# The second layer's input projection in Strassen pairs only, its right side made during the output tiles

## The reference, cut to what matters

```python
h = rms_norm(x, norm_g)
c_q, c_kv, k_rope, z = jnp.split(
    h @ w_in, [Q_LORA, Q_LORA + KV_LORA, Q_LORA + KV_LORA + QK_ROPE], axis=-1)   # 768, 256, 32, 1024 columns
q = (rms_norm(c_q, q_lat_g) @ w_uq).reshape(B, S, MLA_HEADS, QK_HEAD)
...
k = jnp.concatenate([k_nope, jnp.broadcast_to(k_rope[:, :, None, :], ...)], axis=-1)
q = rope_tail(rms_norm(q, q_head_g), cos, sin)
k = rope_tail(rms_norm(k, k_head_g), cos, sin)
o = causal_attention(q, k, v)
return x + (o * jax.nn.silu(z)) @ w_out
```

## Time and profile before

| what | us |
|---|---|
| median of 3 runs | 961.72 (961.34 to 962.45) |
| span of the profiled execution | 960.9 |
| PE busy | 947.5 |
| DVE busy | 812.9 |
| ACT busy | 575.2 |
| POOL busy | 353.1 |

### The profile page before, as it was taken

One profiled execution on the slowest core, in us unless ns is written; L12 is line 12 of the kernel. 1 busy time (PEld: TensorE's weight loads), 2 busy tenths in 40 slices (PEclk: granted clock), 3 DMA queues, 4 the chain that ended last, 5 costly groups with the idle time before them and its releaser, 6 DMA issues.

```text
span 960.9 us, 17257 instructions
## 1 busy us (share of the span) xinstructions
PE 947.5 (99%) x6406; PEld 671.3 (70%) x6406; DVE 812.9 (85%) x1410; ACT 575.2 (60%) x1076; POOL 353.1 (37%) x393
## 2 busy tenths in 40 slices
PE   9999999999999999999999999998999999999998
PEld 8788544444688887644457999996788888887443
DVE  5798899899865579988887899998999999998763
ACT  6443544424434454454646888866899989997230
POOL 0002233222000002235412577875652478894220
PEclk9999999999999999999999999999999999999999
DMA  9320422111054422332123264566676775460231
GB/s 305 45 61 23 110 77 56 44 45 45 1 175 155 152 67 67 107 112 58 31 72 111 89 205 150 204 181 176 119 163 145 171 150 122 82 179 2 88 110 65
DMA packets 165347, 103.74 MB, mean 108 GB/s; under 512 B 75272, under 2 KB 149520, under 8 KB 165008
## 3 DMA queue, kind: packets, MB, share of 16 engines
q1 hardware_dynamic: 159216, 102.25, 38.0%
q10 hardware_dynamic: 6048, 0.39, 0.5%
HBM read 56.48 MB, written 29.36 MB: 89 GB/s over the span
## 4 chain that ended last, share of the span: by engine, by line
PE 72%; DVE 19%; POOL 3%; issue 3%; ACT 2%; DVEq 0%; POOLq 0%; ACTq 0%
PE banks L111 19%; PE banks L113 19%; PE banks L112 19%; PE banks L2728 7%; PE banks L2746 2%; PE banks L2748 2%; PE banks L2747 2%; DVE heads_y L2480 1%; POOL heads_prod L2616 1%; DVE heads_x L2476 1%; DVE heads_x L2475 1%; DVE front_lt L1223 1%; DVE heads_ss L2522 1%; PE banks L2756 1%; DVE front_l L1223 1%
## 5 line engine op out<-in xcount | busy, mean ns | idle before, releaser
L2497 DVE TENSOR_TENSOR heads_pt_lo<-banks,heads_pt_hi 128x512 f16<-128x512 f32 (+2 forms) x192 | 102.1, 554 | 10.8 <-ACT heads_pt_hi L2360 7.8
L2360 ACT ACTIVATE heads_pt_hi<-banks 128x512 f16<-128x512 f32 (+2 forms) x192 | 89.1, 487 | 9.1 <-PE banks L2728 8.9
L2748 PE MATMUL banks<-heads_v,heads_pt_lo 128*128 128x64 f16 x576 | 71.1, 194 | 0.0
L2747 PE MATMUL banks<-heads_v,heads_pt_hi 128*128 128x64 f16 x576 | 71.0, 194 | 0.0
L2489 DVE CUSTOM_DVE_ANT_0 heads_probs_big<-banks,heads_mask,score_scale 128x1024 f32<-128x1024 f32 (+1 forms) x64 | 68.6, 1072 | 2.9 <-PE banks L113 2.7
L2746 PE MATMUL banks<-heads_v,heads_pt_hi 128*128 128x64 f16 x576 | 70.9, 194 | 0.0
L2728 PE MATMUL banks<-ident,heads_probs_big 128*128 128x128 f32 x416 | 69.5, 281 | 1.2 <-ACT heads_probs_big L2351 1.1
L2351 ACT ACTIVATE heads_probs_big<-heads_probs_big,heads_neg_max 128x1024 f32<-128x1024 f32 (+1 forms) x64 | 63.4, 990 | 8.8 <-DVE heads_neg_max L2489 7.7
L111 PE MATMUL banks<-heads_k_t,heads_q_t 96*128 96x512 f16 (+2 forms) x192 | 63.0, 328 | 1.0 <-DVE heads_neg_max L2489 1.0
L111 PE MATMUL banks<-front_act_hi,front_w_hi 128*128 128x512 f32 x160 | 63.8, 399 | 0.0
L113 PE MATMUL banks<-front_act_hi,front_w_lo 128*128 128x512 f32 x160 | 62.4, 390 | 0.0
(11 more groups left out here) (489 smaller groups left out, 3114.5 us busy)
## 6 DMA issues: line engine op xcount, KB each, us to landing
qk_scratch<-heads_y SPq DMA_DIRECT2D x22, 512.0 KB, 3.7
front_x<-in_x_t SPq DMA_DIRECT2D x16, 512.0 KB, 5.3
front_raw<-in_w_in_ab SPq DMA_DIRECT2D x14, 512.0 KB, 5.1
qk_scratch<-heads_last_y SPq DMA_DIRECT2D x10, 512.0 KB, 3.8
front_w<-in_w_out_ab SPq DMA_DIRECT2D x8, 512.0 KB, 3.9
x_scratch<-front_x SPq DMA_DIRECT2D x8, 512.0 KB, 3.9
v_scratch<-heads_v SPq DMA_DIRECT2D x32, 128.0 KB, 3.0
heads_v_st<-v_scratch SPq DMA_DIRECT2D x8, 512.0 KB, 5.2
```

The costliest lines, as they stand in the source:

```text
L2360: nc.scalar.activation(pt_hi[:, q % PIECES, :width], t_ps[:, banks[("piece", n, k)] % 3, :width], ACT.Copy).then_inc(pt_high, 1)
L2497: nc.vector.tensor_tensor(pt_lo[:, q % PIECES, :width], t_ps[:, banks[("piece", n, k)] % 3, :width], pt_hi[:, q % PIECES, :width], ALU.sub ...
L2747: nc.tensor.matmul(o_part, pt_hi[:, q % PIECES, blk], v2[e][:, j, VH:], start=False, stop=False)
L2748: last = nc.tensor.matmul(o_part, pt_lo[:, q % PIECES, blk], v2[e][:, j, :VH], start=False, stop=(j == i))
```

## The change

All of the gate's tiles are made in pairs: two early gate pairs (8 and 9) stand ahead of the four latent pairs (now 10 to 13), and the last two are 14 and 15. The plain tiles 16 to 20 are gone. The right forms are made during the output tiles, two chunk halves at a time (`MADE_AT`), with POOL making most of their sums. Their scale no longer comes from the largest value but from a bound on it, of the norms of x, y and the output weights, that is known ahead of the output tiles (`weight_norm`, `y_norm`, `later_scaling`, one matmul after tile 9). The token sums and the spread of the roots move into pair 8. The rotary keys are made per 128 tokens by products of the right forms (as weights) with the 32 columns' high and low parts (64 or 32 columns wide), after the fourth product of pair 9 (`rotated_keys`). Row sum 8 stands in tile 14, its maximum behind DVE's work on tile 13. A raw pair is loaded by four DMAs instead of two. Some small tiles move, and the areas of the latents, the gate and the right forms change places.

```diff
-    Z0 = OUT0 + OUT_TILES
-    ROPE0 = Z0 + PLAIN_GATES
-    TILES = ROPE0 + 1
-    GATE_PAIRS = PAIRED + LAT // 2
+    TILES = OUT0 + OUT_TILES
+    LAT0 = PAIRED + EARLY_GATES // 2
+    GATE_PAIRS = LAT0 + LAT // 2
...
+    MADE_AT = {2 * c: [(c, SMALL_PART)] + ([(c - 1, T1_PART + n) for n in (1, 2, 3)] if c else []) + [(c, T1_PART)]
+               for c in range(CHUNKS)}
+    MADE_AT |= {2 * c + 1: [(c, WIDE_PART)] for c in range(CHUNKS - 1)}
+    MADE_AT[NK - 1] = [(CHUNKS - 1, T1_PART + 1), (CHUNKS - 1, WIDE_PART), (CHUNKS - 1, T1_PART + 2), (CHUNKS - 1, T1_PART + 3)]
...  (ACT)
                 snapshot(p, 2)
+                weight_norm(p)
...
+            for k in range(NK):
+                y_norm(k)
...
+        def weight_norm(j):
+            slot = norm_in[j % NORM_SLOTS]
+            act.wait_ge(norm_loaded[j % NORM_SLOTS], 16 * (j // NORM_SLOTS + 1))
+            nc.scalar.activation(slot[:], slot[:], ACT.Square, accum_out=norms[:, NK + j:NK + j + 1]).then_inc(norm_squared, 1)
+        def y_norm(k):
+            act.wait_ge(y_high, NK)
+            if k:
+                act.wait_ge(norm_squared, NK + k)
+            nc.scalar.activation(norm_in[0][:], f32(y_hi[:, k, :]), ACT.Square, accum_out=norms[:, k:k + 1]).then_inc(norm_squared, 1)
...
+        for m in range(OUT_TILES):
+            if m and OUT0 + m + 2 < TILES:
+                high(OUT0 + m + 2)
+            act.wait_ge(evacuated, OUT0 + m + 1)
...
+            nc.scalar.activation(xg_of(m)[:], x1[m % RING][:], ACT.Copy, scale=gam1[:, m:m + 1]).then_inc(xg_ready, 1)
+            if m < NK - 1:
+                x1_square(m)
+            rights(m)
+            if m == OUT_TILES - 2:
+                pair_forms(PAIRED, range(FORMS))
         later_paired()
...  (POOL)
         for p in range(PAIRED):
             left_sums(p)
+        for c in range(CHUNKS - 1):
+            right_sums(c, range(4))
         for p in range(PAIRED, ALL_PAIRS):
             left_sums(p)
+            if p == PAIRED:
+                right_sums(CHUNKS - 1, [0])
...  (DVE)
+        for m in range(OUT_TILES):
+            n, x1_m = OUT0 + m, x1[m % RING]
+            if m == 0:
+                low(n + 2)
+            elif m > 1 and n + 1 < TILES:
                 low(n + 1)
+            dve.wait_ge(x1_in[m % RING], 16 * (m // RING + 1))
+            dve.wait_ge(proj_ready, n + 1)
+            nc.vector.tensor_tensor(x1_m[:], proj[:, ring_bank(n)], x1_m[:], ALU.add).then_inc(evacuated, 1)
+            if m == 0:
+                later_scaling()
+            if m < NK - 1:
+                rights(m)
+                if m:
+                    add_x1_square(m)
             else:
+                last_sums()
+            if m == OUT_TILES - 3:
+                pair_peak(PAIRED)
+            if m == OUT_TILES - 2:
+                pair_scale(PAIRED)
+                pair_low(PAIRED, range(FORMS))
         later_paired()
...
+        def first_later_pair():
+            rights(NK - 1)
+            add_x1_square(NK - 1)
+            pair_peak(PAIRED + 1)
+            roots(2, ms1, rstd1, tmp1, sums[:, 0])
...
+            quarter(PAIRED, 0)
+            quarter(PAIRED, 1)
+            pair_scale(PAIRED + 1)
+            pair_low(PAIRED + 1, range(4))
+            quarter(PAIRED, 2)
+            pair_low(PAIRED + 1, range(4, FORMS))
...  (PE)
+                    if n == OUT0 + OUT_TILES - 2 and c == 0 and k == 2:
+                        row_sum(PAIRED)
...
+            pe.wait_ge(mixed, GROUPS)
+            pe.wait_ge(norm_squared, 2 * NK)
+            nc.tensor.matmul(pooled[:, BANK:BANK + K_ROW + 1], ones[:], norms[:], start=True, stop=True).then_inc(bound_spread, 1)
...
-                    if p + 1 < ALL_PAIRS and i == 2:
+                    if p + 1 < ALL_PAIRS and i == (4 if p == PAIRED else 2):
                         row_sum(p + 1)
+                    if p == PAIRED and i == 2:
+                        pe.wait_ge(x1_added, OUT_TILES - 1)
+                        pe.wait_ge(scale_set, PAIRED + 1)
+                        token_sums()
                     if p == PAIRED and i == 3:
+                        spread_roots(2, sums[:, 0])
+                    if p == PAIRED + 1 and i == 3:
+                        rotated_keys()
...
+            for t in range(NT):
+                half, cols = t * P // BANK, slice(t * P % BANK, t * P % BANK + P)
+                whole = slice(t * P, (t + 1) * P)
+                terms = []
+                for c in range(CHUNKS):
+                    terms += [(later_small[c][:, part, cols], 2 * c, part) for part in range(2)]
+                    if half:
+                        terms += [(later_t1[part][:, c, cols], 2 * c, part) for part in range(2)]
+                    terms += [(later_wide[c][:, part, whole], 2 * c + 1, part) for part in range(2)]
+                for j, (tokens, k, part) in enumerate(terms):
+                    width = ROPE if part else 2 * ROPE
+                    last = nc.tensor.matmul(turned_ps[:, t, :width], tokens, wr[:, k, :width], ...)
```

More of the change, by code:

```diff
@@ L259, in front @@
[L259 to L265, removed]
+    xg = [row(f"xg{n}", place) for n, place in enumerate((7, 9, 5, 8))]
@@ new lines, in front @@
+    forms_at = arena + 16 * ROW
+    later_small = [at(f"l11_{c}", [P, 2, BANK], F16, forms_at + c * (ROW // 2)) for c in range(CHUNKS)]
+    later_wide = [at(f"l2_{c}", [P, 2, S], F16, forms_at + (2 + c) * ROW) for c in range(CHUNKS)]
+    later_t1 = [at(f"lt1_{part}", [P, CHUNKS, BANK], F16, forms_at + (6 + part) * ROW) for part in range(2)]
+    later_t = at("lt", [P, 3, 2, CHUNKS, BANK], F16, forms_at + 8 * ROW)
+    stage = [at(f"stage{n}", [P, BANK], F32, w_place + place * ROW + n % 2 * (ROW // 2)) for n, place in enumerate((10, 10, 1, 1))]
@@ L420, in raw_landed @@
     def raw_landed(eng, p):
-        eng.wait_ge(raw_in[p % 2], 32 * (p // 2 + 1) + (0 if p % 2 else 32))
+        loads = sum(4 if q == 0 or q >= PAIRED else 2 for q in range(p % 2, p + 1, 2))
+        eng.wait_ge(raw_in[p % 2], 16 * loads)
     def left_sum(p, n):
@@ L869, in later_paired @@
                 if p == PAIRED:
-                    plain_silu(PLAIN_GATES - 1)
+                    x1_square(NK - 1)
+                if LAT0 <= p < LAT0 + 2:
+                    for i in range(2):
+                        early_silu(2 * (p - LAT0) + i)
                 if p == GATE_PAIRS - 1:
@@ L1243, in plain_gate, with last_sums, add_x1_square @@
-        def plain_gate(i):
-            dve.wait_ge(proj_ready, Z0 + i + 1)
+        def last_sums():
+            dve.wait_ge(xg_ready, NK)
+            dve.wait_ge(t_added, STAGED0 + 4 * (CHUNKS - 1) + 1)
+            for n in (1, 2, 3):
+                t_sum(dve, nc.vector, CHUNKS - 1, n)
+        def add_x1_square(m):
+            dve.wait_ge(x1_squared, m + 1)
+            if m > 1:
+                dve.wait_ge(x1_added, m - 1)
+            nc.vector.tensor_tensor(sums[:, 0], sums[:, 0], x1_sq[:], ALU.add).then_inc(x1_added, 1)
@@ L1429, in vector @@
-        later_scaling()
-        low(Z0 + 1)
-        right_sums(0)
-        right_sums(1)
-        rights(0, range(2))
-        roots(2, ms1, rstd1, tmp1, sums[:, 0])
-        rights(0, range(2, SIX))
-        low(Z0 + 2)
-        right_sums(2)
-        rights(1)
-        plain_gate(0)
-        low(Z0 + 3)
-        right_sums(3)
-        rights(2)
-        plain_gate(1)
-        low(ROPE0)
-        pair_peak(PAIRED)
-        plain_gate(2)
-        rights(3)
-        pair_scale(PAIRED)
-        pair_low(PAIRED, [0])
@@ L1464, in product @@
             hi, lo = operands(n)
-            if n == ROPE0:
-                out, both_parts = proj[:, ring_bank(n), cols], weight(n, 1)[:, k]
-                nc.tensor.matmul(out, both_parts, hi[:, k, cols], start=first, stop=False)
-                return nc.tensor.matmul(out, both_parts, lo[:, k, cols], start=False, stop=last)
             return three_passes(nc, proj[:, ring_bank(n), cols], weight(n, 1)[:, k], weight(n, 2)[:, k],
@@ L1607, in later_paired, with rotated_keys @@
                                          top_diag[0:VGROUPS, :], start=True, stop=True).then_inc(top_spread, 1)
+        def rotated_keys():
+            pe.wait_ge(rstd_set, 2)
+            pe.wait_ge(wr_low, 1)
+            for t in range(NT):
[9 more added lines that the diff above has]
+                    width = ROPE if part else 2 * ROPE
+                    last = nc.tensor.matmul(turned_ps[:, t, :width], tokens, wr[:, k, :width], start=j == 0,
+                                            stop=j == len(terms) - 1, skip_group_check=True)
+            last.then_inc(turned_in, 1)
         def pool_map(g):
@@ L2867, in big @@
             return nc.alloc_sbuf_tensor_at(name, list(shape), dt, offset=base + n * BIG)
-        latent, gate = big(3, "latent"), big(2, "gate")
+        latent, gate = big(1, "latent"), big(0, "gate")
         w_shape = (P, NK, NK, P)
```

446 lines of the change are left out of this document (216 added, 230 removed).

## The result

The changed kernel takes 977.34 us, the kernel before beside it 961.75 (medians of four runs each): ratio 1.0156, 95% interval 1.0143 to 1.0168. That is +15.6 us where +10.3 was forecast; the time lies inside the range, near its upper end.

A forecast was written before the change was run, and what follows sets the result against it. PE was taken to bound the kernel, busy 99% of the span, so its waits are paid whole. −11.9 of PE work, +18.4 of waits and +3.8 of clock gave +10.3 on 961.7: 972 us, 8-in-10 range 963 to 979.

The forecast's parts named there:

- PE's own work: Plain tiles out, two pairs and 160 short products in: −11.9 us if PE never waits.
- (a): PE waits 0.6 us for norms at the bound's matmul after tile 9, and 0.55 at a first-layer row sum.
- (b): Tile 11: PE waits 2.1 us for its weights' low part on DVE; POOL's sums add 0.8 in all.
- (c): Tile 14: pair 8's row sum waits 8.0 us for a maximum standing on DVE after all of tile 13's work.
- (d): Pair 8: the third product waits 5.3 us for ACT's first snapshot; the roots' spread waits 1.0.
- (e): PE's granted clock is lowered after the waits of 8.0 and 5.3: 3.8 us in all, bounds 0 and 6.
- Rival 1: PE's count decides, (c) and (d) not paid: 955 us, the faster side; chance 0.14.
- Rival 3: Short products pay for their weight loads, 0.09 us each instead of 0.029: 9.8 more, 982 us; chance 0.04.
- Rival 2: The waits are right but the clock stays high: 968 us; chance 0.08.
- partly absorbed by the root wait: Pair 8: of the clock loss behind the 5.3 us wait, part falls into the wait for the roots; no separate size.

The follow-up runs named there:

- Experiments 1: Changed kernel with PE's row sum of the pair's peaks issued in output tile 15 instead of tile 14: 965.85 us, ratio 1.0041 to the kernel before.
- experiment 6: Changed kernel with DVE taking the pair's maximum right behind the evacuation of tile 13, PE's order unchanged: 969.73 us.
- the last version: The reordered version of experiment 8 with three more moves in pair 8 (roots' spread, its copy, second snapshot): 952.03 us, ratio 0.9897 to the kernel before.
- experiment 7: Changed kernel with POOL's last three sums of each chunk held until DVE has made the next tile's low part: 972.05 us.
- experiment 5: Changed kernel with 16, 42 and 24 unread matmuls on PE ahead of tile 11, the row sum and pair 8's third product: 974.51 us.
- experiment 2: Changed kernel with ACT's snapshot for pair 8 made ahead of the last output tile's evacuation: 977.49 us.
- experiment 8: Changed kernel with row sum, snapshot, low parts, maximum, last evacuation, bound's matmul, token sums and spread reordered, nothing added or removed: 954.82 us, ratio 0.9927 to the kernel before.

## Why the prediction came out as it did

The steps against the trace of the changed kernel, in the stretch that grew by 16.3 (“remainder” is what is left of it when the waits and the clock are taken off):

| step | forecast | measured |
|---|---|---|
| PE's own work | −11.9 | −11.0 (remainder) |
| (a) bound's matmul; first layer | 0.6 + 0.55 | 0.99 + 0.3 |
| (b) tile 11, POOL | 2.1 + 0.8 | 3.6 |
| (c) row sum in tile 14 | 8.0 | 9.3 |
| (d) third product; spread | 5.3 + 1.0 | 5.4 + 0.9 |
| (e) clock | 3.8 | 2.9 + 1.9 + 2.3 = 7.1 |
| sum | +10.3 | +16.6, of it 0.3 ahead of the stretch |

**Right: that it is slower, and why.** The two large waits stand where they were put, within 1.3 us. The releaser of the first is the one named; for the second the profile names none, and the snapshot's end 0.1 us before bears it out. The pairs end at 529.05 where 523 was forecast. Experiments 1 and 6 show that (c) was the order on PE's and on DVE's queue. Rival 1 falls, and with it what spoke for it: that PE waited hardly anywhere before said nothing of an order that did not yet exist. Rival 3 falls: 160 short products took 407.39 − 403.03 = 4.36 us, 0.027 each. The latent pair has its old 18.27.

**PE's count** was right to 1 us. The two 18.27 pairs and the short products fit; the remainder holds what each stall costs beyond its wait. The gap ahead of tile 11 is 3.98 between starts, that is 0.16 more than the wait and a matmul's 0.23. In the last version, with hardly a stall, the stretch is 502.73 − 254.75 = 247.98: 10.1 less than before, and with its waits in pair 8 (0.88, 0.31 and 0.18) it would be 11.5, so the −11.9 is borne out within half a microsecond.

**(a)** The bound's matmul waited 0.99, not 0.6, because the eight squares came every 1.24 us, not every 1.19. The 0.55 in the first layer is not borne out: in the profiles of seven of the nine experiments the output tiles begin at 253.3 to 254.0, before the old 254.40; the 0.3 of the table is this execution's.

**(b) and (c): POOL was under-sized.** I had a slowed DVE sum in hand and spread 0.8 us over all places. It was 1.5 at tile 11 (3.59 against 2.12) and 1.4 in tile 14 (9.26 against 7.85), and experiment 7 shows that these were POOL's. DVE's pass is not slowed in proportion, it stands still while POOL's instruction runs. In the profile of experiment 5 a DVE operation on 128x8 numbers (0.17 elsewhere) took 1.28, from 371.64 to 372.92, while POOL had a sum from 371.63 to 372.90; the next took 1.18, to 374.14, with POOL's next ending at 374.12. It goes both ways: beside DVE's low part ahead of tile 11, a sum of POOL's that otherwise takes 1.3 us took 2.06. Not every operation is held: the maximum kept its 2.27 beside POOL, and so did one that reads PSUM in the first layer (`y`, 128x1024, 1.27 us from 182.60, beside a sum of POOL's from 182.49). The Trainium skill, SBUF — State Buffer, "SBUF: two separate sides", says that the port pair these engines share is locked for a whole instruction, against a VectorE operation in a two-port mode or with two SBUF inputs. The low parts and the squares' sum have two such inputs, and their durations agree; the operation of 1.28 us in experiment 5 has one, and no run shows in which mode it ran.

**(e) The clock is the term that was furthest off:** 7.1 us where 3.8 stood. I charged it to the waits of 8.0 and 5.3 alone. Tile 11's wait, 2.1 + 0.8 in the forecast, became 3.6 and lowered the clock for 6.8 us, 2.9 of loss; at 2.12 us (experiment 7) it did not. The two errors are coupled: 1.5 us of POOL brought 2.9 of clock. How much clock a wait costs is not fixed: with the same wait of 3.6 ahead of tile 11, experiments 1 and 6 had 3.4 us of low clock and lost 1.8. And the low stretches lasted 6.8, 10.2 and 6.8 us where the earlier trace rows had 3.4. Rival 2, a high clock, falls. The forecast that the loss in pair 8 is partly absorbed by the root wait is not borne out: DVE waits for PE's token sums before the roots, so a slow third product delays the roots as much as PE, and the wait of 0.92 absorbs nothing. Experiment 5 took away those 2.3 and gained nothing in the pair, but for another reason, POOL's sums, which then fell beside the roots. What keeping the clock up gained there was the 4.5 at the tiles less 1.5 in the pair, 3.0; that 3.8 lies near it is luck.

**(d)** had the right wait and the wrong cure: I named the snapshot, and the snapshot was only the last of three that were late (experiment 2). All hang on tile 15's evacuation, which stands behind seven low parts. The split of those is one of several moves in experiment 8, by which pair 8 became 30.7 − 27.7 = 3 us shorter; it was not tried alone, so this cause is read from the queues and not shown by an experiment of its own.

The changed work itself is worth having: with an order of instructions made for it, it is 9.7 us faster than the kernel before, in which PE has only 0.37, 0.58 and 1.03 us of waits in this stretch that another order could save.

## What to carry to other kernels

When work is replaced, count the matmuls saved and then write out every in-order queue beside them: here 12 us of saved matmuls stood against 28 us of stalls and low clock, and moving instructions, with none removed, gave 25 of them back. Put an instruction whose input is long there (a low part of later weights, a maximum) ahead of one that waits for another engine, not behind it. Before curing the instruction that ends a wait, see what comes after it on the other queues: where three are late together, curing the first alone gains nothing. And work that is moved earlier can fall beside another engine that holds it up, as the roots did beside POOL.

## What the runs showed that I had not expected

- The length of a stall does not say what the clock will cost. Stalls of 9.3, 3.6, 2.2 (experiment 6) and 1.8 us (experiment 8, the roots) had a low stretch of the granted clock with them, stalls of 2.1 (experiment 7) and 1.8 us (experiment 8, the fourth product) had none. The low stretch lasted 3.4 or 6.8 us for the same 3.6, and 10.2 or 13.7 for the same 9.3.
- Several DVE operations with their data in SBUF stand still while POOL adds: 1.28 became 1.69, 1.22 became 2.28, 0.17 became 1.28. The maximum kept its 2.27.
- Products of 64 and 32 columns of f16, each with new weights of 128x128, came every 0.027 us, 160 in 4.36.
